# Where the merge stage's transposes stand in TensorE's order: ahead of a tile's products, or behind three of their four groups

## The reference, cut to what matters

```
wts = jax.nn.softmax(jnp.stack(lses, axis=0), axis=0)
od = jnp.sum(wts[..., None] * jnp.stack(outs, axis=0), axis=0)      # mix of the three dilated groups
br_dil = od.reshape(B, S, -1) @ w_br_dil                            # 512 -> 1024
br_mem = om.reshape(B, S, -1) @ w_br_mem                            # 512 -> 1024
gt = jax.nn.sigmoid(gates.reshape(B, S, N_BRANCH, D))
merged = gt[:, :, 0] * br_gla + gt[:, :, 1] * br_dil + gt[:, :, 2] * br_mem
h = x + merged @ w_out
y = h + peer(rms_norm(h, ln2_g))                                    # experts
```

## Time and profile before

| | |
|---|---|
| median of three runs | 4957.4 us (4951.67 to 4961.51) |
| span of the profiled execution | 4949.3 us (its total time is not listed) |
| TensorE busy, whole span | 4241.5 us, 86% |
| VectorE, ScalarE, GpSimd busy | 51%, 36%, 30% |
| merge stage, about 1935 to 2155 us | 220 us |
| experts, about 2155 to the end | 2794 us |

### The profile page before, as it was taken

How to read it: one execution, slowest core, us unless ns; L and a number is a source line. 1 busy time by engine, 2 the same in 40 slices (tenths; PEclk the granted TensorE clock), 3 DMA queues, 4 the chain that set the end, 5 groups by cost and what they waited for, 6 DMA issues and landing times.

```text
span 4949.3 us, 55849 instructions
## 1 busy us (share of the span) xinstructions
PE 4241.5 (86%) x18768; PEld 2558.6 (52%) x18768; DVE 2517.7 (51%) x5454; ACT 1774.2 (36%) x4676; POOL 1491.0 (30%) x1435
## 2 busy tenths in 40 slices
PE   6999999996565887679889889888898898988997
PEld 5888888885434654344434334344344343443361
DVE  3111111116641663346666666666666666666645
ACT  3111111114511553214444444444444444444433
POOL 0000000003620541114444434444344444444433
PEclk9999999997677998889999999999999999999989
DMA  7799898873356774449999999999999999999979
GB/s 263 259 321 316 297 324 273 303 257 104 121 208 259 244 227 142 172 186 421 420 421 418 411 421 406 421 417 412 420 413 412 419 408 420 415 409 417 409 299 386
DMA packets 317397, 1642.02 MB, mean 332 GB/s; under 512 B 43832, under 2 KB 85657, under 8 KB 175225
## 3 DMA queue, kind: packets, MB, share of 16 engines
q0 software_dynamic: 164720, 1168.36, 57.6%
q1 hardware_dynamic: 116464, 248.64, 14.9%
q10 hardware_dynamic: 35984, 222.30, 13.5%
HBM read 1550.39 MB, written 318.03 MB: 378 GB/s over the span
## 4 chain that ended last, share of the span: by engine, by line
DMA 30%; PE 18%; ACT 4%; issue 3%; POOL 1%; DVE 0%; DVEq 0%; POOLq 0%; SPq 0%; ACTq 0%; PEldq 0%
DMA ex_rows<-scratch_uv,ex_E 30%; PE ex_ps_y L2571 13%; PE ex_ps_q L2540 3%; PE ex_ps_t L2503 2%; ACT ex_diag L2296 1%; ACT ex_w L2288 1%; POOL ex_rows L2233 1%; ACT L2284 1%; ACT L2279 1%; ACT ex_gel L2284 1%; PE ex_ps_y L2565 0%; PE ex_ps_s L2553 0%; ACT L2255 0%; ACT L2253 0%; DVE ex_dots L2437 0%
## 5 line engine op out<-in xcount | busy, mean ns | idle before, releaser
L2571 PE MATMUL ex_ps_y<-ex_rows,ex_diag 128*128 128x512 f32 (+1 forms) x4224 | 2019.9, 614 | 312.9 <-ACT ex_diag L2296 293.1
L2437 DVE CUSTOM_DVE_ANT_0 ex_rows<-ex_rows,ex_n2u 128x1024 f32<-128x1024 f32 x1056 | 1294.3, 1226 | 939.4 <-DMA ex_rows<-scratch_uv,ex_E 931.0
L2233 POOL DMA_INDIRECT ex_rows<-scratch_uv,ex_E x1056 | 1136.0, 1076 | 1686.5 <-PE ex_ps_y L2571 1540.3
L2571 PEld LDWEIGHTS ex_ps_y<-ex_rows,ex_diag 128*128 128x128 f32 (+1 forms) x4224 | 749.3, 190 | 1475.6 <-ACT ex_diag L2296 744.7
L344 PE MATMUL pj_ps<-pj_w_hi,pj_nT 128*128 128x470 f32 x3072 | 699.3, 378 | 23.4 <-DVE pj_w_lo L233 12.9
L2284 ACT ACTIVATE ex_gel<-ex_dots 128x1 f32<-128x1 f32 x1056 | 214.0, 203 | 1355.4 <-DVE ex_dots L2437 1354.3
L344 PEld LDWEIGHTS pj_ps<-pj_w_hi,pj_nT 128*128 128x128 f32 x3072 | 580.1, 189 | 109.0 <-issue 29.3
L248 DVE COPY pj_zo<-pj_ps 128x470 f32<-128x470 f32 x96 | 61.4, 646 | 723.3 <-PE pj_ps L344 489.0
L2296 ACT ACTIVATE ex_diag<-ex_ident,ex_w 128x128 f32<-128x128 f32 x1024 | 411.1, 401 | 33.6
L344 PE MATMUL pj_ps<-pj_w_lo,pj_nT 128*128 128x470 f32 x1536 | 361.1, 377 | 0.0
L248 ACT COPY pj_zo<-pj_ps 128x470 f32<-128x470 f32 x96 | 51.9, 553 | 827.8 <-PE pj_ps L344 492.3
(11 more groups left out here) (368 smaller groups left out, 3685.0 us busy)
## 6 DMA issues: line engine op xcount, KB each, us to landing
pj_w<-in_w_in POOLq DMA_DIRECT2D x24, 1880.0 KB, 18.5
scratch_z<-pj_zo SPq DMA_DIRECT2D x192, 235.0 KB, 11.1
scratch_uv<-in_peer_u ACTq DMA_DIRECT2D x8, 4096.0 KB, 26.0
scratch_uv<-in_peer_v ACTq DMA_DIRECT2D x8, 4096.0 KB, 44.1
scratch_uv<-in_peer_u ACTq DMA_DIRECT2D x4, 8192.0 KB, 41.4
scratch_uv<-in_peer_v ACTq DMA_DIRECT2D x4, 8192.0 KB, 70.5
out_dk_s<-in_cache_dil_k ACTq DMA_DIRECT2D x8, 4088.0 KB, 44.3
out_dv_s<-in_cache_dil_v ACTq DMA_DIRECT2D x8, 4088.0 KB, 56.1
```

Source lines behind the costliest of these rows:

```text
L2233: pool.indirect_dma_start(out=rows[:, p % SLOTS, :], out_offset=None, in_=d["uv"], in_offset=bass.IndirectOffsetOnAxis(ap=E[:, turn % 4, k ...
L2437: nc.vector.tensor_tensor_reduce(out=row, in0=row, in1=n2u[:, tile % 2], scale=1.0, scalar=0.0, op0=ALU.mult, op1=ALU.add, accum_out=dots[ ...
L2571: last = nc.tensor.matmul(y[0:n, 512 * c:512 * c + 512], diag[:, p % DIAGS, 0:n], rows[:, p % SLOTS, D + 512 * c:D + 512 * c + 512], start ...
```

## The change

The call `turned(t + 1)` leaves the loop over tiles and goes into `branches(t)`, ahead of its fourth group. Nothing else differs.

```
@@ -2087,6 +2087,8 @@
                     b, c = 1 + q // 2, q % 2
                     i = NPRD * t + q
                     k0, k1 = BRANCH[b]
+                    if q == 3 and t + 1 < N:
+                        turned(t + 1)
                     pe.wait_ge(aT_out, t + 1)
                     if i >= BANKS:
                         pe.wait_ge(gated, i - BANKS + 1)
@@ -2098,8 +2100,6 @@
             pe.wait_ge(wb_in, 48)
             turned(0)
             for t in range(N):
-                if t + 1 < N:
-                    turned(t + 1)
                 branches(t)
```

## The result

The changed kernel takes 4899.08 us (4897.54 to 4902.54, 4 runs) against 4956.97 (4951.67 to 4961.51, 4 runs): ratio 0.9887, 95% interval 0.9875 to 0.9899. That is 56 us less by the ratio (50 to 62), 57.9 by the medians; forecast were 4898.5 us and 58.9 us saved. A second set of runs, in a later session, gave 0.9892 (0.9875 to 0.9908).

The account below looks back on a forecast made before the run. TensorE in the merge was taken to wait each tile for the mix of a tile ahead. Savings 54.5 + 11.2 + 1.2 - 8.0 = 58.9 us gave 4898.5 us, range 4887 to 4912.

Parts of the forecast that it names:

- the stall: Ahead of tile 3's transposes: the first burst of loads lands late beside the cache copies; 8.0 us lost, once.
- the start: Tile 0 of the merge: first products no longer wait for the second tile's transposes; 11.2 us saved.
- TensorE waits for a tile ahead: Merge: TensorE idles 6.98 us for the next tile's mix while the present tile's weights are ready.
- the ring through the mix: Merge loop of last gate, mix, transposes, products: 23.90 us before; rival of a late mix, 40 us saved, shared chance 0.12.
- The mixed tile is there in time: Mix ends 8.1 us after a tile's last product (T), TensorE reaches the transposes at T+10.3: 2.2 us spare.
- Price of a tile: Merge tile: 13.72 us of products plus 1.10 of transposes, 14.82 against 23.91; six tiles save 54.5 us.
- The rival on the clock: TensorE's clock falls at each tile's transposes: 2.3 us a tile, 45 saved, 4912 us; chance 0.04.
- even share: DMA queues of copies and first burst share evenly: burst through at 1991; copies first, 1995 to 1997; 1993 taken.
- Tile 7: Merge tile 7: from 15.48 us to 13.72 and some 0.6; 1.2 us saved.
- Loads that set the pace: Merge: gate-value transfers of 15 us and more give tiles of 16 to 17; 43 to 50 saved; shared chance 0.12.
- Given back by the experts: Experts stage, DMA at 0.98, gives back what the merge saves; result 4957 us; chance 0.04.
- Slower: Merge: bursts longer than 23.9 us make the fourth group wait in every tile; about 4962 and up; chance 0.02.

Follow-up runs that it names:

- behind four: Changed kernel with the next tile's transposes behind all four groups of products instead of three; 4900.0 us, ratio 0.9891 to the kernel before.
- behind two and one: Changed kernel with the next tile's transposes behind the second, or the first, group of products; 4900.7 us (0.9897) and 4922.6 us (0.9940).
- more ScalarE work: Changed kernel with a ScalarE copy of the gates onto themselves ahead of the sigmoid in each tile; 4903.2 us, ratio 0.9903.
- the same again: The changed kernel run once more with nothing altered; 4897.0 us, ratio 0.9892 to the kernel before.
- first tile as before: Changed kernel, but tile 1's transposes stand ahead of tile 0's products as in the kernel before; 4898.0 us, ratio 0.9890.
- issued at tile 4: Changed kernel with GpSimd's cache copies issued at tile 4 of the merge instead of tile 1; 4901.2 us, ratio 0.9900.
- issued at tile 7: Changed kernel with GpSimd's cache copies issued at tile 7 of the merge instead of tile 1; 4884.9 us, ratio 0.9860.

## Why the prediction was right, point by point

In short: the wait was the one named, the new tile came out within 0.2 us, and the one stall stood where it was forecast. Mis-sized were the stall (8.0 us forecast, 9.4 measured) and the start (11.2 and 9.8), and what the start is worth turned out to hang on the copies.

**TensorE waits for a tile ahead.** Right. With the call moved the idle of the earlier trace rows is gone. The runs behind four, three, two and one group give tiles of 16.03, 14.61, 14.92 and 20.05 us, with a least at three: behind four the copy is uncovered, behind two and one the ring through the mix closes again.

**The mixed tile is there in time.** Right: forecast T+8.1 with 2.2 us spare, measured 8.1 and 2.0, the latter also by the run with more ScalarE work.

**Price of a tile.** 14.82 forecast, 14.61 measured. The transposes, taken at 1.10, cost 1.04 us as rows but only 0.88 to the next product (2044.07 to 2044.95), and the clock stayed at 1.00. The rival on the clock is out.

**The sum, tile 0 to tile 6.** Forecast 54.5 - 8.0 = 46.5 us. Measured: 143.47 before, 2063.19 - 1966.18 = 97.01 after, 46.5 saved. That it is the same to a tenth is luck, since two errors cancel: the tiles gave 6 x 9.30 = 55.8, and the stall took 23.97 - 14.61 = 9.4.

**The stall.** Its place, cause and kind are shown: tile 3, the copies, the burst. The size was 8.0 forecast and 9.4 and 11.7 measured. The step that was off is the burst's landing. I had taken 1993, between an even share (1991) and the copies first (1995 to 1997); counted from the stage's start, 59.7 us, the loads were in at 1936.15 + 59.7 = 1995.8 on the clock of the profile before. The even share that gave 1991 was one of bytes, and that was my step. What the Trainium skill states ("DMA: Bandwidth & Descriptors", section on queues, rings and completion order) is turns by packet, and with that the trace agrees, if the packets that it counts are those. From 1972 to 1984, with the copies and the bursts in both queues, the changed kernel's trace counts 339 packets of the copies and 350 of SP's queue; but of the first 39 and 43, up to 1976, the copies' hold 0.97 MB and SP's 0.18. Over the whole stretch it is 2.12 against 1.82 MB, and part of SP's is burst 1, in the queue from 1982.23 on, before burst 0 was in. So what failed in the landing, which came 2.8 us later than I had taken it, is the share between the queues: I had left out the sizes of the packets and burst 1. The runs do not separate the two. A slip of no consequence: by the prediction's own terms tile 2 would end at 1998.4 + 1.9 + 4.9 = 2005.3, not 2006.7.

**The start.** Forecast 11.2; measured 42.66 - 32.87 = 9.8 us from the stage's first issue to tile 0's last gate. The low clock lasted for 5.9 us of products, 1948.49 to 1954.37: six records some 0.86 us apart and a seventh at 0.60, where before it were three and a fourth at 0.54, and there the second tile's transposes (1.94 us at the low clock) had run just ahead of them. The sum stays right, since its idle was taken as landing less arrival and so has the earlier arrival in it; but as a reading of what the start is worth it misleads. Up to tile 3 the merge is bound by the DMA: it is full (1.01 from 1967.6 to 1993), and the burst was in at 59.7, 60.8, 61.0 and 59.7 us behind the stage's start in the changed kernel, the same again, first tile as before and behind four, though issued up to 11 us apart. So start and stall are not two effects. Take the start away and 0.7 us are lost, not 11.2: a later start only makes the stall shorter.

**Tile 7.** Forecast 1.2, measured 15.48 - 14.54 = 0.9.

**Sum.** 46.5 + 9.8 + 0.9 = 57.2, the merge's difference, against 58.9; the merge was to be about 161 us and is 162.6.

**Rivals.** Loads that set the pace: only at tile 3; in quiet tiles of the changed kernel no load is waited for. Given back by the experts: no, the times follow the merge (above). Slower: no.

## What to carry to other kernels

Put the work for the next tile behind as much of the present tile's work as it takes for its inputs to be ready, and ahead of as much as it takes to cover what follows from it; the place can be worked out from two times, when the input comes and how long the copy behind it takes. Before adding two gains of one stage, ask whether a transfer lies across both: here 10 us at the start were worth 0.7 or nothing until the copies were moved. And a stage that becomes shorter needs its side traffic looked at again: copies that cost nothing in tiles of 23.9 us cost 9 to 11 us of merge in tiles of 14.6 (16 when issued at tile 4), and issued at tile 7 they made no tile longer.

## What the runs showed of the hardware that was not expected

- With 1.16 us of idle per tile TensorE's clock stayed at 1.00. With 3.55 us it mostly fell, at a varying place: the transposes right behind took 1.06 to 1.57 us, and a tile cost 1.9 us more; in one tile of that run it stayed at 1.00 and the price was nil.
- Eight transposes of 128x128 at the high clock cost 0.88 us between products; at the low clock it is 1.73 (2105.33 to 2107.06).
- Beside the copies the store of 512 KB took 12.4 us (8.1 before, 2.9 in a quiet tile), and the issue of a load of the next burst held SP for 3.54 us instead of 0.43 (at 1982.61, while the first burst was still in flight). With the copies at tile 4 two issues in a row held it for 7.40 and 7.96 us (2011.67, 2019.11).
- With transfers in both queues the trace counts nearly as many packets of the one as of the other (364 and 348 in 8 us), with very unlike bytes (2.06 and 0.66 MB).
- Experts of identical code differed by 7.8 us between profiles, more than most of the differences under study.
